# A hybrid decoder step: first-chunk tables formed on GpSimd, six half gate units computed later, a residual tile transposed unscaled

## What is computed

```python
h = rmsnorm(x, norm_mix)
u_s5, x_lru, y_lru, g_a, g_b = split(h @ w_in)         # 512, 512, 512, 1024, 1024 channels
a_out = s5_branch(u_s5, ...)    # complex diagonal scan over time, then z * sigmoid(z @ w_glu + b_glu)
b_out = rglru_branch(x_lru, y_lru, ...)                # causal conv, gated linear scan
merged = sigmoid(g_a) * (a_out @ w_proj_a) + sigmoid(g_b) * (b_out @ w_proj_b)
x = x + merged @ w_out
x = x + peer(rmsnorm(x, norm_ffn), w_q, sub_keys, u_tab, v_tab)
y = rmsnorm(x, norm_final)
```

## Time and profile before

| | us |
|---|---|
| median of 3 runs (3053.35 to 3057.33) | 3056.95 |
| the profiled execution's own time | 3054.68 |
| its span, first to last instruction | 3052.7 |
| first gather issued, from the span's start | 188.89 |
| mean DMA rate over the span | 398 GB/s, 1215.48 MB |

### The profile page before, as it was taken

How to read it: one execution, slowest core, us unless ns; L and a number is a source line. 1 busy time by engine, 2 the same in 40 slices (tenths; PEclk the granted TensorE clock), 3 DMA queues, 4 the chain that set the end, 5 groups by cost and what they waited for, 6 DMA issues and landing times.

```text
span 3052.7 us, 43457 instructions
## 1 busy us (share of the span) xinstructions
PE 2438.8 (80%) x14644; PEld 1173.8 (38%) x14644; DVE 2162.9 (71%) x5371; ACT 1204.3 (39%) x3783; POOL 1115.4 (37%) x1048
## 2 busy tenths in 40 slices
PE   9997768899876778888877768899977776667675
PEld 7864324455333324455333324455433331111111
DVE  7757887776479876676468987676558897554445
ACT  2224444433345444333335444333244444333333
POOL 0023443333334443333334443333334344433332
PEclk9998878999998889999988879999998886676667
DMA  4569999999999999999999999999999999999998
GB/s 156 199 243 398 414 414 419 419 415 416 413 421 411 419 418 420 421 409 421 420 420 402 418 418 413 421 418 420 417 418 414 409 411 415 421 421 421 420 421 343
DMA packets 176079, 1215.48 MB, mean 398 GB/s; under 512 B 22360, under 2 KB 22744, under 8 KB 31472
## 3 DMA queue, kind: packets, MB, share of 16 engines
q0 software_dynamic: 148608, 1082.20, 85.9%
q1 hardware_dynamic: 25744, 126.19, 10.4%
q10 hardware_dynamic: 1504, 4.33, 0.4%
HBM read 1208.12 MB, written 4.51 MB: 397 GB/s over the span
## 4 chain that ended last, share of the span: by engine, by line
DMA 29%; issue 23%; PE 19%; DVE 14%; POOL 11%; ACT 3%; DVEq 0%; ACTq 0%; POOLq 0%; SPq 0%
DMA arena<-in_uv,arena 16%; DMA arena<-in_vu,arena 13%; POOL arena L802 11%; PE psum L2273 8%; DVE arena L1825 6%; PE psum L2161 4%; DVE arena L1307 3%; PE psum L2317 2%; ACT arena L856 2%; DVE arena L1315 1%; PE psum L2337 1%; PE psum L2349 1%; ACT L856 1%; DVE arena L1582 0%; DVE arena L1688 0%
## 5 line engine op out<-in xcount | busy, mean ns | idle before, releaser
L1825 DVE CUSTOM_DVE_ANT_0 arena<-arena 128x1024 f32<-128x1024 f32 x1024 | 1246.6, 1224 | 770.3 <-DMA arena<-in_uv,arena 371.9
L2273 PE MATMUL psum<-arena 64*64 64x512 f32 x8184 | 1286.6, 731 | 559.0 <-ACT arena L856 494.8
L856 ACT ACTIVATE arena<-arena 128x1 f32<-128x1 f32 (+3 forms) x3252 | 931.9, 289 | 1628.8 <-DVE arena L1825 1447.7
L802 POOL DMA_INDIRECT arena<-in_vu,arena x517 | 550.7, 1065 | 998.0 <-DVE arena L1825 690.6
L802 POOL DMA_INDIRECT arena<-in_uv,arena x515 | 561.6, 1090 | 917.6 <-DVE arena L1825 800.9
L2273 PEld LDWEIGHTS psum<-arena 64*64 64x64 f32 x8184 | 275.8, 150 | 1374.8 <-ACT arena L856 1060.3
L2161 PE MATMUL psum<-arena 128*128 128x256 f32 (+1 forms) x2656 | 643.2, 398 | 3.4 <-DVE arena L1315 1.7
L2161 PEld LDWEIGHTS psum<-arena 128*128 128x128 f32 x2656 | 511.8, 197 | 200.6 <-issue 123.9
L1307 DVE TENSOR_TENSOR arena<-arena 128x256 f32<-128x256 f32 (+11 forms) x562 | 250.0, 471 | 12.9 <-ACT psum L856 0.8
L856 ACT ACT_TABLE_LOAD x119 | 152.7, 1283 | 11.0 <-DVE arena L1307 7.0
L856 ACT ACTIVATE arena<-psum 128x256 f32<-128x256 f32 (+5 forms) x254 | 98.8, 402 | 119.1 <-PE psum L2161 75.9
(11 more groups left out here) (139 smaller groups left out, 1039.2 us busy)
## 6 DMA issues: line engine op xcount, KB each, us to landing
arena<-in_w_in SPq DMA_DIRECT2D x56, 1024.0 KB
arena<-in_w_q SPq DMA_DIRECT2D x34, 1024.0 KB
arena<-in_vu,arena POOLq DMA_INDIRECT x517
arena<-in_uv,arena POOLq DMA_INDIRECT x515
arena<-in_w_ab SPq DMA_DIRECT2D x11, 512.0 KB, 11.5
arena<-in_keys SPq DMA_DIRECT2D x17, 256.0 KB, 14.8
arena<-in_w_out SPq DMA_DIRECT2D x8, 512.0 KB, 16.2
arena<-in_x_tok SPq DMA_DIRECT2D x8, 512.0 KB
```

The lines of the kernel that those rows point to most:

```text
L802: pool.indirect_dma_start(rows_[:, first:first + 2 * D], None, table, bass.IndirectOffsetOnAxis(column, 0)).then_inc(uv_in[at % UV], 16)
L856: return nc.scalar.activation(out, in_, f, **kw)
L1825: V.tensor_tensor_reduce(out=u, in0=u, in1=hn, scale=1.0, scalar=0.0, op0=ALU.mult, op1=ALU.add, accum_out=dots_[:, b % DOTS, k:k + 1]).th ...
L2273: ins = mm(PV[o:o + HP, half], dg[r:r + HP, PAIR * (b % 2) + k], cells[r:r + HP, v_cell(place(c, i)), at:at + 512], start=(i % (SLOT // 2) ...
```

## The change

Three edits, all in the first chunk. (1) The 18 table operations move from VectorE (`for half ...` and `c_tables`) to a new function `tables()` on GpSimd. It starts at `set_b` (the sines), and its last six wait for `bp_ok`. VectorE waits for the first 12 before its first scan step, TensorE for all 18 before the first `s5_out`, SyncE for all 18 before it loads a weight into cell 2. (2) The gate units m = 10 to 15 are computed for the early 128 columns in their place, and for the late 128 columns behind `head(0, ...)` and `row_everywhere`. Their six weight blocks are parked in cells 9, 10, 12, 13, 2 and 5 in between, and the three parked `w_ab` move to cells 14, 11 and 8. (3) The second tile's residual is transposed as it is, ScalarE and VectorE multiply by `nffnT` while they take it out, and the inverse root is applied to its scores; `scale(1, 1)` and the second `row_everywhere` go.

```diff
-MIX_CELLS = (13, 14, 12)
+MIX_CELLS = (14, 11, 8)
+LATE_W = tuple(("w_in", U_GATE + m) for m in LATE_GATES)      # LATE_GATES = (10, 11, 12, 13, 14, 15)
+LATE_CELLS = (9, 10, 12, 13, 2, 5)
...
+                    if weight(0, l) == LATE_W[4]:
+                        sp.wait_ge(table_ok, TABLES)
+                        sp.wait_ge(s5_ok, 1)
...
+            def tables():
+                tt = nc.gpsimd.tensor_tensor
+                done = 0
+                pool.wait_ge(set_b, 2)
+                for half in range(SJ // HJ):
...
+                    for dst, (p0, p1), (p2, p3), op in ((cosT, (1, 1), (0, 0), ALU.subtract),
+                                                        (sinT, (0, 1), (1, 0), ALU.add)):
+                        need(pool, table_ok, done)
+                        tt(b4[0], small(p0, 0), small(p1, 1), ALU.mult).then_inc(table_ok, 1)
+                        tt(b4[1], small(p2, 0), small(p3, 1), ALU.mult).then_inc(table_ok, 1)
+                        pool.wait_ge(table_ok, done + 2)
+                        tt(dst[:, js], big, big2, op).then_inc(table_ok, 1)
+                        done += 3
...
+                pool.wait_ge(bp_ok, 1)
...
-                    tt(b4[0], small(p0, 0), small(p1, 1), ALU.mult)      # on VectorE, the same 12
...
-            def c_tables():
...
+                        elif held & set(LATE_CELLS):
+                            pool.wait_ge(unit, U_LATE + 1 + max(k for k, cell in enumerate(LATE_CELLS) if cell in held))
...
-                        project(c, ga_unit(c, m), U_GATE + m, hT[c], KT, n)
+                        project(c, ga_unit(c, m), U_GATE + m, hT[c], KT, P if m in LATE_GATES else n)
...
                 row_everywhere(PBf, nffnT, nf_ok)
+                pe.wait_ge(glu_ev, QT + 2)
+                for i, m in enumerate(LATE_GATES):
+                    w = slot(0, U_GATE + m)
+                    if i >= 2:
+                        pe.wait_ge(evac, U_MIX0 + 1 + i)
+                    for t in range(KT):
+                        ins = mm(SB[i % 2][:, 0:P], w[:, P * t:P * t + P], hT[0][:, t, late], ...)
+                    ins.then_inc(unit, 1)
...
+                upto(OLD + 5)
+                for half, done in ((0, tr0_ok), (1, tr_ok)):
+                    pe.wait_ge(x2_ok, 3 + half)
+                    for k in range(KT // 2 * half, KT // 2 * half + KT // 2):
+                        ins = transpose(k, 1, PSf)
+                    ins.then_inc(done, 1)
                 upto(OLD + 6)
-                pe.wait_ge(x2_ok, 4)
-                row_everywhere(PBf, nffnT, nf_ok)
-                pe.wait_ge(hn_ok, 2)
-                transposes(0, 1, P, lambda k: psum[:, 4 + k // 4, ...]).then_inc(tr_ok, 1)
```

More of the change, by code:

```diff
@@ L797, in _, with small, over @@
                           allow_small_or_imprecise_dtypes=True).then_inc(const_ok, 1)
+            def tables():
[3 more added lines that the diff above has]
+                for half in range(SJ // HJ):
+                    js = slice(HJ * half, HJ * half + HJ)
+                    def small(part, axis, js=js):
+                        v = sc[:, part, js, 0:TA] if axis == 0 else sc[:, part, js, TA:TA + TB]
+                        return v.unsqueeze(3 if axis == 0 else 2).to_broadcast([P, HJ, TA, TB])
+                    b4 = [x.rearrange("p j (a b) -> p j a b", a=TA) for x in (big, big2)]
+                    for dst, (p0, p1), (p2, p3), op in ((cosT, (1, 1), (0, 0), ALU.subtract),
[6 more added lines that the diff above has]
+                        done += 3
+                def over(a):
+                    return a.unsqueeze(2).to_broadcast([P, SJ, 32])
+                pool.wait_ge(bp_ok, 1)
+                for part, (x, y, op) in enumerate(((0, 1, ALU.add), (1, 0, ALU.subtract))):
+                    pool.wait_ge(table_ok, done)
+                    tt(c0, over(a_re), craw[:, x], ALU.mult).then_inc(table_ok, 1)
+                    tt(c1, over(a_im), craw[:, y], ALU.mult).then_inc(table_ok, 1)
+                    pool.wait_ge(table_ok, done + 2)
+                    tt(cT[:, part], c0, c1, op).then_inc(table_ok, 1)
+                    done += 3
+                pool.wait_ge(table_ok, done)
+            tables()
             def gather(at, column):
@@ L1143, in mixing_gate @@
                         act.wait_ge(lru_ok, QT * c + m + 1)
-                    af(dst, PB[u % 2][:, 0:n], ACT.Tanh, scale=0.5).then_inc(evac, 1)
+                    k = P if first and m in LATE_GATES else n
+                    af(dst[:, 0:k], PB[u % 2][:, 0:k], ACT.Tanh, scale=0.5).then_inc(evac, 1)
                 if first:
```

139 lines of the change are left out of this document (72 added, 67 removed).

## The result

The changed kernel takes 3067.09 us (median of 6 runs, 3065.96 to 3069.56), the kernel before 3056.25 beside it (6 runs): ratio 1.0038, 95% interval 1.0028 to 1.0048. That is 10.8 us slower. I had forecast 4 us slower and a range up to 3067: the direction was right, the size was not, and the time lies 0.1 us beyond the range. The interval of the medians' difference reaches from 8.6 to 14.7 us.

A forecast was written before the change was run, and what follows sets the result against it. Bound: a start, a transfer-bound body with DMA full at about 420 GB/s, a short end. 3 us before the first scores plus 1 behind made 4 more: 3054.68 to 3058.7, median 2.3 above, 3061.0; range 3046 to 3067.

The forecast's parts named there:

- The lock: While VectorE forms bp, each of GpSimd's first 12 table operations holds up one of VectorE's for 1.1 us; bp_ok 11 us late.
- First scores 3 us later: Start of the first chunk: last s5_out 4.7 us later, less 1.7 for the short last unit, so first scores 3 us later.
- the short last unit gives 1.7 back: Behind the last s5_out: TensorE's last gate unit, now on 128 columns, is 1.7 us shorter.
- rival 2: Same lock at 1.3 us or more an operation, +6 to +7, plus 1 to 2 for TensorE's clock: 3065; chance 0.22.
- Behind the first scores: Late gates, 11 us, delay the first dots by 9 us; sixth gather waits, 6 us of transfer idle time; net 1 us lost.
- the making-up: From 255 to 282 us, where VectorE is the bound in head 2's list, 5 of the 6 us idle time come back.
- Rival 3: Idle time behind the first scores not made up, 6 in place of 1, with half the lock's delay: 3060; chance 0.10.
- The unscaled transposes: Second tile, before head 2: first query 5 us after the residual instead of 11; counted inside the net 1 us lost.
- Rival 1: VectorE is not held by GpSimd's tables: first scores 8.1 us earlier, less 1 lost behind: 3050; chance 0.32.

The follow-up runs named there:

- memsets: Changed kernel with GpSimd's first 12 table operations replaced by memsets of the same areas, writing without reading; 3055.62 us, +2.7 against before, one execution.
- copies: Changed kernel with GpSimd's first 12 table operations replaced by one-input copies of the same size; 3059.28 us, +6.3 against before, one execution.
- changed, dots moved: Changed kernel with VectorE's first two steps of dots moved up, ahead of the late mixes and between their halves; 3062.14 us, +8.5 against before.
- two and three, scans and dots moved: scans_early with VectorE's first three steps of dots ahead of, between and behind the late mixes; 3048.60 us, -4.4 against before.
- scans_early: Edits two and three, tables on VectorE, the last four pieces of the other branch moved behind the last scan step; 3053.45 us against 3052.97 before.

## Why the prediction was right or wrong, step by step

**The lock: right, and to the place.** Forecast: `bp_ok` at 56, the scan from 72, the fifth step at 102.8, operations of 1.1 us. Measured: transposes of `bp` at 56.10, scan at 71.11, fifth step at 102.98, operations of 1.05 to 1.33 us. The rows on gathers beside dots carried this, and the memsets and copies show that it is reading that does it. In both places where the tables were tried on GpSimd, at the sines and behind `bp`, the first gather came later than with the tables on VectorE (by 7.2 and by 1.9 us, beside edits two and three).

**First scores 3 us later: too small.** The last `s5_out` was forecast 4.7 us later and is 5.3 (140.75 for 135.47). The step that failed here is the one behind it, "the short last unit gives 1.7 back". The unit gave nothing back: TensorE had been idle for 3.23 us, `s5_out` then took 1.81 us in place of 1.07 and the short unit 2.91 in place of 1.9. In the window from 140 to 145 us the granted clock is 0.66, where it was 1.00 at that place before. The glu stands 5.2 us later than before, the first gather 5.9. I had priced the clock only in rival 2, and only for the hole at 45 us. It does not fall each time: with the memsets, behind the same pause (3.21 us), the window from 134 to 136 us has 1.00, `s5_out` takes 1.07 us and the unit 2.05. From the start of the last `s5_out` to the glu it is 2.9 us in two of the nine traces with such a pause (2.2 to 4.5 us) and 4.3 to 4.5 in the seven others, and no row shows what decides. So of the 5.9 us some 1.6 could have been absent in another execution.

**Behind the first scores: the place right, the making-up wrong, and this is the step that failed.** Late gates 10.88 us (forecast 11), sixth gather 17.7 us behind the first (16), idle time 5.8 us in the hole (6) and 7.7 with its tail. Then I wrote "I put 5 of the 6 us back", because VectorE is the bound from 255 to 282 us. That did not happen. The stretch of low rates moved with its cause: the list of head 2 starts at 266.50 instead of 255.43, and the four low windows are at 280 to 300 us (287, 374, 338, 395) instead of 265 to 285 (335, 302, 360, 344). They miss 290 x 5 / 421 = 3.4 us where they missed 4.1. So 0.7 us came back by these windows and 0.5 by the bytes moved, not 5. A list stands in VectorE's program behind a fixed number of dots, and each dot behind its gather; between 255 and 265 us the transfers run at 423 and VectorE waits for them 1.3 to 3.6 us before a dot. So the list does not find its transfers done ahead of time, and most of what was missed before it stays missed. Edits two and three alone (+5.3) and moving the dots (-2.4 in the changed kernel, -4.9 beside the earlier scans) show the same from both sides. How much comes back differs, though. By the bytes moved, us behind the kernel before:

| kernel | at 55 MB | at 75 MB | medians |
|---|---|---|---|
| changed | 13.6 | 13.1 | 10.8 |
| first edit | 13.3 | 14.9 | 12.6 |
| edits two and three | 6.6 | 5.0 | 5.3 |
| second edit | 7.3 | 5.6 | 6.7 |
| third edit | -0.2 | -2.4 | -3.1 |
| changed, dots moved | 11.8 | 8.2 | 8.5 |
| two and three, scans and dots moved | -1.6 | -5.3 | -4.4 |

The second edit alone gets 1.7 us of its loss back, the moved dots 3.6, the changed kernel 0.5, and the first edit, which has no hole, loses 1.6 more in that stretch. No run tells what sets this. With the measured terms in place of mine the sum is 5.9 + 7.7 - 0.5 = 13.1 us; the medians say 10.8, with 13.1 inside the interval.

**Rival 3** had this very mechanism, at a chance of 0.10, but joined to half of the lock. What came was the whole lock together with idle time that is not made up, and no case of mine held both. The range was built from cases in which one of them went wrong at a time. Rival 2's 3065 lies closer to 3067.09 than my forecast, but not for its reason: it needed 1.25 us an operation, and GpSimd's first 12 took about 1.15.

**The unscaled transposes: the time right, the worth not.** First query of head 2 at 245.29, 4.7 us behind the residual at 240.61 (forecast 5), 50.5 us behind the first gather (forecast 51). But I had let the edit count only as a part of the making-up. Alone it is worth 3.1 us, since the list of head 2 then takes less from the transfers; beside the late gates the traces show 0.6.

**Rival 1, had it come, was sized too high.** The memsets let `bp` through with 0.5 us of delay, and the first gather gained 3.4 us (185.44), not 8.1, although the clock did not fall there. Its fifth scan step started at 95.27: 1 us earlier than the 96.3 of before, as TensorE's pace allows, and not at the 91.8 that I had written in the sentence behind that very pace.

**The account of the 10.8 us.** Edits two and three make 5.3 of it (second alone 6.7, third alone -3.1), and the first adds 5.5 to them by the medians. The traces say 8.1 for the first (13.1 behind in place of 5.0), 7.2 of it ahead of the first gather. Alone the first costs 12.6, so the three do not add: the shortened units hide part of the hole that the first one makes.

## What to carry to other kernels

Work moved to an engine that shares a way into SBUF with the one it relieves is priced by turns, not by engines: look for what the relieved engine does at that time, count its two-input operations, and charge each the full length of the other's instruction, however small it is. Where transfers are the bound, do not count on a later low stretch to make up their idle time: here every consumer stands behind a fixed number of transfers, the low stretch moved with the delay, and most of the loss stayed. When TensorE is given less to do, look at once for who is late next, and reorder that engine too: the second and third edits together lost 5.3 us until VectorE's scans and dots stood earlier, and gained 4.4 with them. And before a gain of 1 or 2 us between two traces is put down to an edit, look whether the place that gained lies behind it at all.

## What the runs showed of the hardware that I had not expected

**`tensor_scalar` operations with one input are held too, and by writes.** In the changed kernel three one-input operations on 4 elements took 2.59 us in place of 0.67. Beside memsets, which left the two-input operations alone, the same three took 1.29 us, and the one ahead of them 0.68 in place of 0.17:

```profile
27.87 0.68 DVE L1366 TENSOR_SCALAR arena<-arena 128x4 f32<-128x4 f32 x1
28.63 1.86 DVE L1370 SCALAR_TENSOR_TENSOR arena<-arena 128x4 f32<-128x4 f32 x8
30.56 1.29 DVE L1366 TENSOR_SCALAR arena<-arena 128x4 f32<-128x4 f32 x3
```

The Trainium skill, in the same section of SBUF — State Buffer, states that `tensor_scalar` can enter a 2-port mode, when its operands meet the conditions, and that VectorE in such a mode contends with GpSimd; these rows agree. My working had charged GpSimd's operations to two-input operations alone.

**TensorE's clock could be low behind a pause of 2.2 or 3.2 us as behind one of 10.7, and was not each time.** In the changed kernel the window from 140 to 145 us, behind the 3.23 us of idle time, had a granted clock of 0.66; the one from 56 to 61 us, behind the 10.7, had 0.70, where in the kernel before 45 to 50 us had 1.00. Behind 2.20 us of idle time it was 0.50 from 132 to 134 us in scans_early, and 1.00 behind 2.21 us in the same program with the dots moved. The 128 transposes of `bp` took 3.70 us before, 5.08 in the changed kernel and 6.29 in the run with the first edit alone, behind the same idle time to 0.01 us; why the last two differ no row shows.

**0.6 us between list and gather.** From VectorE's first maximum on the scores of head 0 to the first gather it is 7.6 us in the kernel before and in the six others with the tables on VectorE, and 8.2 us in all six in which GpSimd has operations of `tables()` ahead of its gathers: 186.54 to 194.75 in the changed kernel, 181.31 to 188.89 before, 177.23 to 185.44 with the memsets. It is the difference between 5.2 us at the glu and 5.9 at the first gather. No run tells its cause.
